# The first stage of a hybrid encoder step: its loads in another order, its norm in groups of tiles

## The reference, cut to what matters

```python
mod = silu(c) @ w_ada + b_ada              # c: one vector for the prompt, one for the sample
sh1, sc1, g1, sh2, sc2, g2 = split(mod, 6)
h = x * rsqrt(mean(x * x, axis=-1) + EPS) * (1 + sc1) + sh1
u, q, k, v, qi, ki, wi, gate_a, gate_b = split(h @ w_in)
```

## Time and profile before

| | |
|---|---|
| median of three runs | 1543.55 us |
| profiled execution, its own time | 1545.17 us |
| its span in the trace | 1543.4 us |
| TensorE busy | 1372.2 us, 89% of the span |
| VectorE, ScalarE, GpSimd busy | 817.8, 443.3, 253.4 us |
| mean granted TensorE clock | 0.944 of full speed |

### The profile page before, as it was taken

One profiled execution on the slowest core, in us unless ns is written; L12 is line 12 of the kernel. 1 busy time (PEld: TensorE's weight loads), 2 busy tenths in 40 slices (PEclk: granted clock), 3 DMA queues, 4 the chain that ended last, 5 costly groups with the idle time before them and its releaser, 6 DMA issues. The chain is left out here.

```text
span 1543.4 us, 20736 instructions
## 1 busy us (share of the span) xinstructions
PE 1372.2 (89%) x7461; PEld 797.9 (52%) x7462; DVE 817.8 (53%) x1722; ACT 443.3 (29%) x963; POOL 253.4 (16%) x454
## 2 busy tenths in 40 slices
PE   3899996988989899999959998989992599999994
PEld 2555553666734466666626665644441444544542
DVE  0422222886577788989955555334235444444433
ACT  3321111232355466765135555001111000000000
POOL 0000002003010011111100000000000245555553
PEclk8899998998989999999989999999996599999998
DMA  8500015764031422321050000542326479886752
GB/s 325 182 3 5 32 36 139 226 194 53 11 86 48 145 82 86 127 71 57 30 199 1 2 1 2 203 140 96 109 86 225 146 245 313 279 310 213 245 178 74
DMA packets 141563, 193.04 MB, mean 125 GB/s; under 512 B 33125, under 2 KB 108837, under 8 KB 141253
## 3 DMA queue, kind: packets, MB, share of 16 engines
q1 hardware_dynamic: 120092, 151.43, 29.8%
q0 software_dynamic: 17904, 37.23, 7.5%
q10 hardware_dynamic: 3482, 3.23, 0.8%
HBM read 159.75 MB, written 53.42 MB: 138 GB/s over the span
## 5 line engine op out<-in xcount | busy, mean ns | idle before, releaser
L2270 PE MATMUL ps<-ex_wgu,ex_xT 128*128 x416 | 185.2, 599 | 0.3 <-issue 0.3
L1391 DVE TENSOR_SCALAR_CACHE_REDUCE tk_eq<-sc,tk_cand 128x512 bf16<-128x512 f32 (+4 forms) x155 | 146.8, 1007 | 0.0
L1789 PE MATMUL ps<-hT,mergedT 128*128 128x512 f32 (+1 forms) x288 | 120.1, 600 | 4.9 <-DMA op_wr<-in_w_route_expert 4.9
L2270 PEld LDWEIGHTS ps<-ex_wgu,ex_xT 128*128 128x128 f32 x416 | 77.8, 192 | 89.1 <-issue 89.0
L1325 PE MATMUL ps<-zT,gt_w 128*128 128x352 f32 (+1 forms) x384 | 120.9, 468 | 0.0
L1325 PE MATMUL ps<-hT,gt_w 128*128 128x352 f32 (+1 forms) x336 | 105.8, 468 | 0.0
L1325 PEld LDWEIGHTS ps<-zT,gt_w 128*128 128x128 f32 x384 | 73.0, 190 | 44.0
L2290 PE MATMUL ps<-ex_wd,ex_hidT 128*128 x208 | 93.6, 593 | 2.0 <-DVE ex_hidT L2343 2.0
L1354 ACT ACTIVATE mask<-sc,tk_cand 128x384 bf16<-128x384 f32 (+1 forms) x62 | 82.2, 1329 | 15.0 <-DVE tk_cand L1407 15.0
L1789 PEld LDWEIGHTS ps<-hT,mergedT 128*128 128x128 f32 (+1 forms) x288 | 50.9, 186 | 68.3 <-issue 62.7
L2336 DVE SCALAR_TENSOR_TENSOR ex_hid<-ex_silu,ex_weight,ps 128x256 f32<-128x256 f32 x26 | 12.5, 480 | 135.6 <-ACT ex_silu L2314 135.6
(11 more groups left out here) (484 smaller groups left out, 2282.4 us busy)
## 6 DMA issues: line engine op xcount, KB each, us to landing
ex_wgu<-in_w_gate SPq DMA_DIRECT2D x16, 1024.0 KB, 7.2
ex_wgu<-in_w_up SPq DMA_DIRECT2D x16, 1024.0 KB, 10.1
ex_wd<-in_w_down SPq DMA_DIRECT2D x16, 1024.0 KB, 5.6
sp_ada_w<-in_w_ada SPq DMA_DIRECT2D x9, 1024.0 KB
merge_left_dram<-qiT SPq DMA_DIRECT2D x8, 544.0 KB, 6.4
mg_gb<-gate_b_dram SPq DMA_DIRECT2D x8, 544.0 KB, 3.9
mergedT<-merge_left_dram SPq DMA_DIRECT2D x8, 544.0 KB, 4.9
u<-in_w_ada SPq DMA_DIRECT2D x2, 2048.0 KB, 13.2
```

Of the source, the lines that this page charges most:

```text
L1391: return v.tensor_scalar(junk[j], m.sc[0:r, c:c + w], scalar, 0.0, op, ALU.add, accum_out=cnt[0:r, j:j + 1])
L1789: i = nc.tensor.matmul(m.ps[rows, 2 * (t % 2) + n, :], m.mergedT[:, k, t * P:t * P + r], m.wout[:, k, n * 512:(n + 1) * 512], start=k == 0 ...
L2270: j = nc.tensor.matmul(m.ps[:, 2 + b, :], xT[:, b, k, :], wgu[:, bass.ds(at, 1), k, :].rearrange("p o n -> p (o n)"), start=k == 0, stop=k ...
```

## The change

The nine tiles fall into four groups, `normed = ((0,), (1,), (2, 3), (4, 5, 6, 7, 8))`. Mean, root, reciprocal and scaling are done for a group at a time. The loads go in this order: w0, w1, w2, x0, (wait `ps >= 1`) w3, x1, wq, x2, x3, wr, x4 to x8, wu.

```diff
+        normed = ((0,), (1,), (2, 3), (4, 5, 6, 7, 8))
@@ SyncE
                 for i in range(NB):
                     load_w(i)
-                    for t in range(3 * i, 3 * i + 3):
-                        load_x(t)
+                load_x(0)
                 sp.wait_ge(ps, 1)
                 load_w(NB)
-                for sem, lo, hi in ((wlq, 512, 1024), (wlr, 1024, OFF_GA), (wlu, 0, 512)):
+                load_x(1)
+                for sem, lo, hi, tiles in ((wlq, 512, 1024, (2, 3)), (wlr, 1024, OFF_GA, (4, 5, 6, 7, 8)), (wlu, 0, 512, ())):
                     sp.dma_start(pw[:, :, lo:hi], wp[:, :, lo:hi]).then_inc(sem, 16)
+                    for t in tiles:
+                        load_x(t)
@@ TensorE
                 x_transposes(0)
+                mod_rows(NB)
+                columns(NB).then_inc(colt, 1)
                 pe.wait_ge(gqe, 1)
                 x_transposes(1)
-                mod_rows(NB)
-                columns(NB).then_inc(colt, 1)
+                queries(0)
                 x_transposes(2)
-                queries(0)
+                rest(0)
                 x_transposes(3)
-                rest(0)
+                queries(1)
                 x_transposes(4)
-                queries(1)
-                x_transposes(5)
                 rest(1)
-                for t in range(6, TILES):
+                for t in range(5, TILES):
                     x_transposes(t)
@@ ScalarE
+                def root(k):
+                    for t in normed[k]:
+                        r = rows_of(t)
+                        act.wait_ge(x_in[t], 16)
+                        if t >= 2:
+                            act.wait_ge(ssq, t - 1)
+                        nc.scalar.activation(junk[0:r, t % 2, :], x[0:r, t, :], ACT.Square,
+                                             accum_out=st1[0:r, 0, t:t + 1]).then_inc(ssq, 1)
+                    act.wait_ge(msx, k + 1)
+                    c = slice(normed[k][0], normed[k][-1] + 1)
+                    nc.scalar.activation(st1[:, 2, c], st1[:, 1, c], ACT.Sqrt).then_inc(sr, 1)
...
-                act.wait_ge(dv, 2)
-                nc.scalar.activation(st1[:, 2, :], st1[:, 1, :], ACT.Sqrt).then_inc(sr, 1)
+                root(0)
                 act.wait_ge(ps, n)
...
+                root(1)
                 act.wait_ge(colc, 1)
-                for t in range(5):
-                    evacuate_x(t)
+                evacuate_x(0)
+                evacuate_x(1)
+                root(2)
+                evacuate_x(2)
+                root(3)
+                evacuate_x(3)
                 squares(0)
-                for t in range(5, TILES):
+                for t in range(4, TILES):
                     evacuate_x(t)
@@ VectorE
+                def norm_x(k):
+                    c = slice(normed[k][0], normed[k][-1] + 1)
+                    dve.wait_ge(ssq, c.stop)
+                    v.tensor_scalar(st1[:, 1, c], st1[:, 0, c], 1.0 / D, EPS, ALU.mult, ALU.add).then_inc(msx, 1)
+                    dve.wait_ge(sr, k + 1)
+                    step(v.reciprocal(st1[:, 3, c], st1[:, 2, c]))
+                    for t in normed[k]:
+                        r = rows_of(t)
+                        v.tensor_scalar(x[0:r, t, :], x[0:r, t, :], st1[0:r, 3, t:t + 1], None, ALU.mult).then_inc(xnr, 1)
...
-                dve.wait_ge(ssq, TILES)
-                step(v.tensor_scalar(st1[:, 1, :], st1[:, 0, :], 1.0 / D, EPS, ALU.mult, ALU.add))
-                dve.wait_ge(sr, 1)
-                step(v.reciprocal(st1[:, 3, :], st1[:, 2, :]))
...
+                    if i == NB - 1:
+                        norm_x(0)
+                norm_x(1)
                 dve.wait_ge(colt, 1)
...
-                for t in range(5):
-                    evacuate_x(t)
+                evacuate_x(0)
+                evacuate_x(1)
+                norm_x(2)
+                evacuate_x(2)
+                norm_x(3)
+                evacuate_x(3)
                 normalise(0)
-                for t in range(5, TILES):
+                for t in range(4, TILES):
                     evacuate_x(t)
```

More of the change, by code:

```diff
@@ L125, in norm_and_project @@
             "c_loaded", "c_transposed", "c_silu", "psum_ready", "rows_copied", "columns_transposed", "columns_copied"))
-        ssq, dv, sr, xnr, xt, evd, eva = (m.sem("n1_" + k) for k in (
-            "sumsq", "dve_chain", "root", "xn_ready", "transposed", "evacuated_by_dve", "evacuated_by_act"))
+        ssq, dv, msx, sr, xnr, xt, evd, eva = (m.sem("n1_" + k) for k in (
+            "sumsq", "dve_chain", "mean", "root", "xn_ready", "transposed", "evacuated_by_dve", "evacuated_by_act"))
         wlq, wlr, wlu = (m.sem(f"pj_{k}_weights_loaded") for k in ("q", "rest", "u"))
@@ L436, in _ @@
                     j.then_inc(rowc, 1)
-                dve.wait_ge(ssq, TILES)
-                step(v.tensor_scalar(st1[:, 1, :], st1[:, 0, :], 1.0 / D, EPS, ALU.mult, ALU.add))
-                dve.wait_ge(sr, 1)
-                step(v.reciprocal(st1[:, 3, :], st1[:, 2, :]))
-                for t in range(TILES):
-                    r = rows_of(t)
-                    v.tensor_scalar(x[0:r, t, :], x[0:r, t, :], st1[0:r, 3, t:t + 1], None, ALU.mult).then_inc(xnr, 1)
+                    if i == NB - 1:
+                        norm_x(0)
+                norm_x(1)
                 dve.wait_ge(colt, 1)
```

## The result

The changed kernel takes 1536.73 us (median of six runs, 1535.60 to 1538.91) where the kernel before, run beside it, takes 1547.56: a ratio of 0.9937, with a 95% interval of 0.9921 to 0.9954, 10.8 us by the medians. A later pair gave 1537.58 and 1545.95, 8.4 us, ratio 0.9948 (0.9931 to 0.9964). So it is faster, clear of the 0.3% that the prediction asks for, and by about the 10.75 us forecast; that the first pair agrees to 0.1 us is luck, since its interval alone reaches from 7 to 12 us. The forecast time of 1532.8 was counted from 1543.55, the median then shown; further runs of the kernel before put it 2 to 4 us higher, and so the measured 1536.73 lies 0.7 us above the forecast's own range of 1530.5 to 1536.

What follows compares the result with a forecast made beforehand. The first stage's head was taken as bound by arriving loads and a chain of small steps, then by TensorE from the inputs on. -12.1 + 1.35 = -10.75 us from 1543.55 gives 1532.8 us; own range 1530.5 to 1536.

Steps and rivals of the forecast that it cites:

- Where each load lands: Loads land in order of issue without the DMA engines running dry: w3 at 30.5 us, wq at 38.1.
- w2 at 22.8: Landing of the third chunk's load, which starts its matmuls on TensorE: 22.8 us, or 24.8 at the slower pace; before 32.09.
- I take the row with the same MiB: Landing times taken from the profiled load with as many MiB ahead; for w2, 6 MiB, x3's 22.8 us.
- The chain behind w2: Steps from w2's landing to the first queries, which start at 40.6 us in place of 52.71: -12.1 us.
- The middle, 0: From the first queries to the end of rest(1), TensorE does the same work: 0; first queries kept at 8.89 us.
- The tail, +1.35: From the end of rest(1) to the inputs, four tiles left instead of three: 6.65 us instead of 5.30, +1.35.
- The inputs: First two inputs on TensorE, 15.45 us before; after a longer gap perhaps up to 1.4 more, taken as 0.
- The sum: Total for the kernel: -12.1 + 1.35 = -10.75 us, inputs(0) at 76.9 us, time 1532.8 us.
- Table loads: Rival: ScalarE loads a table at each switch between Square and Sqrt, +2.6 us, 1535.4 us; chance 0.03.
- A late group: Rival: tiles 4 to 8 or tile 4's evacuation come 4 us late, TensorE waits, 1538 to 1541 us; chance 0.08.
- The loads as the bound: Rival: w2, w3 and wq land later, shifting the chain by 2 to 5 us, 1535 to 1538 us; chance 0.11.
- The slower rival: TensorE's clock stays low from 40.6 to 76.9 us: +25.8 less 10.75, 1558.6 us; chance 0.05.

Runs made afterwards that it cites:

- The run with the sized filler: Changed kernel with 36 unused identity matmuls (4, 17, 3, 4, 8) in TensorE's waits ahead of the first queries: 1534.23 us, ratio 0.9921.
- the fastest version: Changed kernel with x1's norm early, tile 5 transposed ahead of rest(1), queries(2) and rest(2) between tiles 6 to 8, and 28 filler matmuls: 1529.48 us, ratio 0.9898.

## Why the prediction was right, step by step

- *Where each load lands.* SyncE's timeline gives the issue of w3 and wq, the DMA view their time to landing: 16.68 + 14.4 = 31.1 and 21.19 + 16.6 = 37.8; forecast 30.5 and 38.1. The DMA engines did not run dry (a share of 1.01 to 1.08 from 10 to 48 us), and the wait `ps >= 1` cleared at 16.68 (forecast 16.4).

```profile
16.68 0.37 SPq L147 DMA_DIRECT2D u<-in_w_ada  x1
...
21.19 0.60 SPq L162 DMA_DIRECT2D pj_w<-in_w_in  x1
```

```profile
u<-in_w_ada SPq DMA_DIRECT2D x1, 2048.0 KB, 14.4
```

```profile
pj_w<-in_w_in SPq DMA_DIRECT2D x1, 2048.0 KB, 16.6
```

- *w2 at 22.8* was the one point that was off: 24.5, near the slow end of its bounds (24.8). "I take the row with the same MiB" failed here, by 1.7 us: x3, the row taken, landed 1.3 us behind w1 before (0.5 MiB, 2.5 us per MiB), whereas the third of three chunks in a row landed 6.7 us behind the second (3.3 per MiB).
- *The chain behind w2* was a little shorter than its terms, which won 0.9 back: strip copies done 4.9 us after the chunk's start (5.3), norm of x0 1.45 (1.6), transposes 1.9 (1.85), fourth chunk with copies 4.1 (4.3), norm of x1 2.6 (2.75). Queries(0) at 41.4 instead of 40.6: -11.3 instead of -12.1.
- *The middle, 0.* 70.73 - 41.38 = 29.35 against 29.6; the first queries 8.64 against 8.89, so the reason for keeping 8.89, little work on TensorE ahead, held: the granted clock was 0.50 from 38 to 44 us and 1.00 from 46. The run with the sized filler shows what the lower clock costs from the third chunk on: the first queries ended 2.9 us earlier.
- *The tail, +1.35.* 6.71 - 5.30 = +1.41, and the run with tile 5 moved back took it away, at the price of 0.87 us ahead of rest(1).
- *The inputs* took 0.34 longer (15.79 against 15.45), inside "up to 1.4 more, taken as 0".
- *The sum.* Inputs(0) 10.2 us earlier (10.75), the next stage 9.84 earlier: w2's 1.7 and the chain's 0.9 were both off, and that they cancelled in part is luck. "Nothing else changes" holds as far as the spread of the later part allows.
- *The rivals.* Table loads: one, as the rows said; the Trainium skill's rule to batch by table set ("ScalarE: Activation LUTs", "Table sets: the hidden batching unit") didn't bite, as no switch of set occurs among the norms (one load ahead of the first at 27.00, 1.28 us, then none in this stage). A late group: none. The loads as the bound: half of it came, w2 at 24.5 against the rival's 24.8, but w3 at 31.1 and wq at 37.8 held nobody up; in the fastest version they do. The slower rival, TensorE staying at 1.2 GHz through 77 us, didn't happen; between 46 and 78 us the clock was at 2.4 GHz.

## What to carry to other kernels

Bring a load forward only together with its consumer: either half of this change alone was worth nothing or cost 14 us. Walk the chain after a reordering as if it were new: an engine's program order had put 2 us of another tile's norm between two steps that don't need it, and left 3 us of evacuation uncovered behind the last matmuls. Count an order by all that it moves: tile 5 ahead of rest(1) took 1.4 us from the tail and put 0.9 in front of it. Where a chain's gaps let TensorE's clock fall, matmuls that nobody needs can shorten it, if they fit into the gaps (2.9 us at the end of the first queries, and nothing in the time when they overran); measure one before counting them.

## What the runs showed of the hardware that was not expected

- The same instructions ran at either level of TensorE's clock from one execution to the next: behind the same loads, landed within 0.3 us of each other, chunk 1, with no filler ahead of it, took 1.93 to 3.59 us, and 3.24 and 3.59 in two executions of the changed kernel itself; the first two inputs took 14.1 to 16.9. A term of 1 to 2 us that lies behind a gap is then not to be read from one profile.
- The granted clock's rows show 1.00 from the start until they first change, near 18 us in the kernel before and 24 in the changed one; yet chunk 0 takes 3.4 to 3.6 us there, as chunk 2 does at 0.50 in the run with x1's norm early, and not the 1.93 seen at 1.00 later. A duration tells the level better than the row does in that stretch.
- One fp32 matmul of the 128 x 128 identity on itself took 0.23 us at 2.4 GHz (30 in 6.96), while a transpose of 128 x 128 took about 0.12 (16 pieces in 1.91). In the trace such a matmul stands as two instructions of 0.12 us (x60 for the 30) and a transpose as one; so do the kernel's other fp32 matmuls, x16 for the eight calls of one tile's queries and x64 for the 32 of a chunk.
